# First mixer of a fused block: stick-breaking sums by a running total on VectorE, retention heads in pairs, gate products on one bank

## The reference, cut to what matters

```
# stick-breaking, 8 heads of 64, query blocks of 128
z = einsum('bthd,bshd->bhts', q, k) * scale
log_one_minus = where(s < t, log_sigmoid(-z), 0)
suffix = cumsum(log_one_minus, reverse=True) - log_one_minus
w = where(s < t, exp(log_sigmoid(z) + suffix), 0)
out = einsum('bhts,bshd->bthd', w, v)

# retention, 4 heads of 64 keys and 128 values
scores = einsum('bhnid,bhnjd->bhnij', rotary(q), rotary(k)) * decay
o = rms_norm(scores @ v + carried state) * silu(rg)
```

## Time and profile before

| | |
|---|---|
| Time, median of 3 runs | 2060.03 us (2060.03 to 2063.84) |
| Time of the profiled execution | 2062.9 us |
| Its span, first to last instruction | 2061.1 us |
| TensorE busy | 1815.9 us, 88% of the span |
| VectorE, ScalarE, GpSimd busy | 951.9, 740.2, 925.8 us |
| Share of the last-ended chain on TensorE | 71% |
| First mixer from the first `sz` to the last `sp` | about 99 to 330 us |

### The profile page before, as it was taken

The page is one execution under the profiler, slowest core; times in us unless marked ns, Lnnn a source line. Parts: engine busy times, 40 slices in busy tenths (PEclk is TensorE's granted clock), DMA queues, the critical chain, the costliest instruction groups (busy, mean ns, idle before and its releaser), DMA issues.

```text
span 2061.1 us, 20065 instructions
## 1 busy us (share of the span) xinstructions
PE 1815.9 (88%) x7492; PEld 1363.4 (66%) x7492; DVE 951.9 (46%) x1451; ACT 740.2 (36%) x1207; POOL 925.8 (45%) x1100
## 2 busy tenths in 40 slices
PE   5999889888878898878999999988777889999996
PEld 4776456666756576455788888755454568888885
DVE  1033333677562599754430323564755554123244
ACT  4253454445344422364332322342232342322232
POOL 3433113464753354113565656468222246565563
PEclk9999999998988899988999999998778899999998
DMA  4211102212111222012233323211000122333231
GB/s 167 92 62 52 41 21 73 70 62 72 50 33 34 69 80 74 21 31 72 73 95 99 102 93 102 82 62 51 11 11 21 31 64 90 103 92 102 93 94 70
DMA packets 39553, 139.90 MB, mean 68 GB/s; under 512 B 4512, under 2 KB 4640, under 8 KB 39328
## 3 DMA queue, kind: packets, MB, share of 16 engines
q1 hardware_dynamic: 39456, 138.61, 21.1%
HBM read 136.50 MB, written 2.10 MB: 67 GB/s over the span
## 4 chain that ended last, share of the span: by engine, by line
PE 71%; DVE 17%; ACT 7%; issue 2%; POOL 1%; DMA 0%; SPq 0%; DVEq 0%; ACTq 0%; POOLq 0%
PE ps L570 18%; PE ps L571 17%; PE ps L572 17%; DVE ps L1689 3%; PE ps L599 2%; PE ps L583 1%; PE ps L2101 1%; PE ps L585 1%; PE ps L584 1%; PE ps L818 1%; PE ps L820 1%; POOL wl L2586 1%; PE ps L2078 1%; ACT wh L624 1%; PE ps L811 1%
## 5 line engine op out<-in xcount | busy, mean ns | idle before, releaser
L2586 POOL TENSOR_TENSOR wl<-raw,wh 128x256 fp32r<-128x256 f32 x988 | 801.7, 843 | 998.7 <-ACT wh L624 990.8
L570 PE MATMUL ps<-hh,wh 128*128 128x512 f32 x1204 | 518.5, 431 | 70.2 <-DVE hl L687 45.8
L571 PE MATMUL ps<-hl,wh 128*128 128x512 f32 x1204 | 479.5, 398 | 0.0
L572 PE MATMUL ps<-hh,wl 128*128 128x512 f32 x1204 | 478.9, 398 | 0.0
L624 ACT ACTIVATE wh<-raw 128x1024 fp32r<-128x1024 f32 x247 | 261.1, 1058 | 554.8 <-PE ps L572 507.5
L570 PEld LDWEIGHTS ps<-hh,wh 128*128 128x128 f32 x1204 | 233.2, 194 | 149.1 <-DVE hl L687 51.8
L570 PE MATMUL ps<-mh,wh 128*128 128x512 f32 x632 | 267.6, 423 | 46.1 <-DVE ml L1324 6.5
L571 PEld LDWEIGHTS ps<-hl,wh 128*128 128x128 f32 x1204 | 232.7, 193 | 61.4 <-issue 17.7
L572 PEld LDWEIGHTS ps<-hh,wl 128*128 128x128 f32 x1204 | 232.1, 193 | 50.8
L571 PE MATMUL ps<-ml,wh 128*128 128x512 f32 x632 | 254.2, 402 | 0.0
L572 PE MATMUL ps<-mh,wl 128*128 128x512 f32 x632 | 253.9, 402 | 0.0
(11 more groups left out here) (464 smaller groups left out, 2297.2 us busy)
## 6 DMA issues: line engine op xcount, KB each, us to landing
raw<-in_w SPq DMA_DIRECT2D x247, 512.0 KB, 3.5
x<-in_x SPq DMA_DIRECT2D x8, 256.0 KB, 6.9
out<-x SPq DMA_DIRECT2D x8, 256.0 KB, 2.0
arena<-in_rope SPq DMA_DIRECT2D x3, 512.0 KB, 4.8
arena<-in_dec SPq DMA_DIRECT2D x1, 1024.0 KB, 11.6
mats<-in_mats SPq DMA_DIRECT2D x1, 576.0 KB, 7.8
arena<-in_lw SPq DMA_DIRECT2D x1, 512.0 KB, 3.8
arena<-in_levels SPq DMA_DIRECT2D x1, 448.0 KB, 4.5
```

Of the source, the lines that this page charges most:

```text
L570: e.matmul(ps[b][:], a, xh, start=first, stop=False)
L571: e.matmul(ps[b][:], a, xl, start=False, stop=False)
L572: e.matmul(ps[b][:], l, xh, start=False, stop=final).then_inc(pe.sem, pe.up(*step))
L2586: e.tensor_tensor(wl[:, n % NHL, cut(i, 2)], raw[:, n % NRAW, cut(i, 2)], wh[:, n % NHL, cut(i, 2)].bitcast(F32), SUB).then_inc(split.sem, ...
```

## The change

1. **Stick-breaking sums.** The -2^100 mask is added to z by VectorE, in the bank, before ScalarE reads it (step `sz`, two additions of 128 columns). Softplus moves into a step `sy` of its own and needs no mask. VectorE keeps the running sum of later key blocks (`later_at`: for n = 2 and 1 one addition and one copy for each lane, in step `ss`). TensorE then needs one `tri` matmul and, for n < 3, one `negones` matmul, and no mask matmul.
2. **Retention by pairs of heads.** `rz` issues both heads of a pair back to back, one on each half of the partitions, into banks 2 and 3; `rv` and `rn` issue both heads too, in banks 7 and 1.
3. **Gate products on one bank.** The `rg` groups all use bank 0, since bank 1 is now taken.
4. **Order.** The retention steps are laid by hand among the gate groups, each group's eviction stands before one more retention step, and the costs in `LONG` and the distances handed to `beside` are new.

```diff
-LONG = {"w": 0.69, "t": 2.8, "ra": 0.9, "rz": 0.6, "rv": 0.6, "rn2": 0.9}
+LONG = {"w": 0.69, "t": 2.8, "ra": 0.9, "rz": 0.5, "rv": 0.9, "rn2": 1.4}
...
-            stick += [[("sz", j, n)] + before, [("ss", j, n)]]
+            stick += [[("sz", j, n)] + before, [("sy", j, n)], [("ss", j, n)]]
...
-    return out + beside(others + part[:-10], stick, 5.4, 2.7) + before + part[-10:] + closing(4)
+    return out + beside(others + part[:-10], stick, 2.8, 2.6, 2.7) + before + part[-10:] + closing(4)
...
-    "even": {... "rg": (0, 1), ...},
+    "even": {... "rg": (0,), ...},
...
 # TensorE, step rz
-                    e.matmul(ps[b][:, 0:T - 128 * i], rqk[2 + j][r, cut(i)], rqk[j][r, 128 * i:T], start=True,
-                             stop=True).then_inc(pe.sem, pe.up(*step))
+                    for lane in range(2):
+                        r = slice(64 * lane, 64 * lane + 64)
+                        e.matmul(ps[2 + lane][:, 0:T - 128 * i], rqk[2 + j][r, cut(i)], rqk[j][r, 128 * i:T], start=True,
+                                 stop=True).then_inc(pe.sem, pe.up("rz", 2 * j + lane, i))
...
 # TensorE, step ss
-                        e.wait_ge(dve.sem, dve["masked", lane, j, n])
-                        e.matmul(z, M("tri"), sp[:, OFF[n]:OFF[n] + T - 128 * n], start=False, stop=False, skip_group_check=True)
-                        for n2 in range(n + 1, 4):
-                            e.matmul(z[:, 128 * (n2 - n):], M("negones"), sp[:, OFF[n2]:OFF[n2] + T - 128 * n2], start=False,
-                                     stop=False, skip_group_check=True)
-                        e.matmul(z[:, 0:128], R("ident"), R("sneg"), start=False, stop=True, skip_group_check=True).then_inc(
+                        e.wait_ge(dve.sem, dve["softplus", lane, j, n])
+                        m = e.matmul(z, M("tri"), softplus_at(lane, n), start=False, stop=(n == 3), skip_group_check=True)
+                        if n < 3:
+                            e.wait_ge(dve.sem, dve["later", lane, j, n] if n < 2 else dve["softplus", lane, j, 3])
+                            m = e.matmul(z[:, 128:], M("negones"), later_at(lane, n), start=False, stop=True,
+                                         skip_group_check=True)
...
 # VectorE
+                        z = ps[4 + lane][:, 0:128]
+                        e.tensor_tensor(z, z, M("sneg"), ADD).then_inc(dve.sem, dve.up("z_masked", lane, j, n))
...
-                        e.tensor_tensor(sp[:, 0:128], sp[:, 0:128], M("smask"), MUL).then_inc(
-                            dve.sem, dve.up("masked", lane, j, n))
+                            e.tensor_tensor(to[:, 128:], sp[:, 128:], later_at(lane, n), ADD).then_inc(
+                                dve.sem, dve.up("later_sum", lane, j, n - 1))
+                            e.tensor_copy(to[:, 0:128], sp[:, 0:128]).then_inc(dve.sem, dve.up("later", lane, j, n - 1))
...
 # ScalarE, step sz
-                        e.wait_ge(pe.sem, pe["z", lane, j, n])
+                        e.wait_ge(dve.sem, dve["z_masked", lane, j, n])
```

More of the change, by code:

```diff
@@ L737, in turned, with softplus_at, later_at @@
             return e_tmp[2 * (j % 2)], e_tmp[2 * (j % 2) + 1]
+        RVB = (7, 1)
+        def softplus_at(lane, n):
+            o = (768, 640, 128, 0)[n]
+            return spb[lane][:, o:o + T - 128 * n]
+        def later_at(lane, n):
+            o = (0, 384, 0)[n]
+            return spb[lane][:, o:o + T - 128 * (n + 1)]
         def scores(h, i):
@@ L780, in pe_even @@
                 elif kind == "rz":
-                    _, h, i = step
-                    b, j, r = 2 + i % 2, h // 2, slice(64 * (h % 2), 64 * (h % 2) + 64)
-                    claim(e, b)
+                    _, j, i = step
+                    claim(e, 2)
+                    claim(e, 3)
                     if i == 0:
                         e.wait_ge(dve.sem, dve["rotated", 2 + j])
-                    e.matmul(ps[b][:, 0:T - 128 * i], rqk[2 + j][r, cut(i)], rqk[j][r, 128 * i:T], start=True,
-                             stop=True).then_inc(pe.sem, pe.up(*step))
@@ L788, in pe_even @@
-                    busy[b] = (dve, ("rz", h, i))
-                elif kind == "rv":
[L790 to L796, removed]
-                elif kind == "rn2":
[L798 to L801, removed]
+                    for lane in range(2):
+                        r = slice(64 * lane, 64 * lane + 64)
+                        e.matmul(ps[2 + lane][:, 0:T - 128 * i], rqk[2 + j][r, cut(i)], rqk[j][r, 128 * i:T], start=True,
+                                 stop=True).then_inc(pe.sem, pe.up("rz", 2 * j + lane, i))
+                        busy[2 + lane] = (dve, ("rz", 2 * j + lane, i))
+                elif kind == "rv":
+                    _, j, i = step
+                    for lane in range(2):
+                        h, b = 2 * j + lane, RVB[lane]
+                        if i == 0:
+                            claim(e, b)
+                            e.wait_ge(act.sem, act["te", "rv", 3])
+                        e.wait_ge(dve.sem, dve["rz", h, i])
+                        e.matmul(ps[b][:, 128 * i:T], rv[:, i, cut(h)], scores(h, i)[:, 0:T - 128 * i], start=(i == 0),
+                                 stop=(i == 3)).then_inc(pe.sem, pe.up("rv", h, i))
+                elif kind == "rn2":
+                    for lane in range(2):
+                        h, b = 2 * step[1] + lane, RVB[lane]
+                        e.wait_ge(act.sem, act["rn_square", h])
+                        e.matmul(ps[b][:], M("ones"), scores(h, 1), start=True, stop=True).then_inc(pe.sem, pe.up("rn2", h))
+                        busy[b] = (act, ("rn_ln", h))
@@ L950, in act_even @@
                 elif kind == "rn1":
[L951 to L954, removed]
-                elif kind == "rn2":
[L956 to L961, removed]
+                    for lane in range(2):
+                        h, b = 2 * step[1] + lane, RVB[lane]
+                        e.wait_ge(pe.sem, pe["rv", h, 3])
+                        e.activation(oret[:, h, :], ps[b][:], ACT.Copy).then_inc(act.sem, act.up("rn_copy", h))
+                        e.activation(scores(h, 1), ps[b][:], ACT.Square).then_inc(act.sem, act.up("rn_square", h))
+                elif kind == "rn2":
+                    for lane in range(2):
+                        h, b = 2 * step[1] + lane, RVB[lane]
+                        e.wait_ge(pe.sem, pe["rn2", h])
+                        e.activation(scores(h, 0), ps[b][:], ACT.Ln, scale=1.0 / 128, bias=C(EPS)).then_inc(
+                            act.sem, act.up("rn_ln", h))
+                    for h in (2 * step[1], 2 * step[1] + 1):
+                        e.wait_ge(act.sem, act["rn_ln", h])
+                        e.activation(scores(h, 0), scores(h, 0), ACT.Exp, scale=-0.5).then_inc(act.sem, act.up("rn_exp", h))
                 elif kind == "ga":
```

76 lines of the change are left out of this document (48 added, 28 removed), and 2 rows, old and new, of the table BANKS.

## The result

| | median | runs | span of the profile |
|---|---|---|---|
| before, measured beside it | 2061.94 us | 2060.03 to 2068.16, 4 | 2061.1 us (the profile of the earlier trace rows) |
| changed kernel | 2041.46 us | 2040.97 to 2044.16, 4 | 2039.4 us |

The ratio is 0.9898, 95% interval 0.9882 to 0.9915: 21 us faster (17.5 to 24.3), where 13.3 were forecast. The median lies at the lower edge of the range, 2041; the ratio on the 2060.03 us that the forecast started from gives 2039.0, outside it. Between the profiles the gain is 21.7 us.

A forecast was written before the change was run, and what follows sets the result against it. TensorE, busy 211.4 of the first mixer's 231 us, was taken as the bound. Work of -16.1 us with changes in waits and clock summed to -13.3, so 2060.0 became 2046.7 us, range 2041 to 2054 (forecast's own 2043 to 2050).

The forecast's parts named there:

- (c): Value evictions: TensorE waits 3.9 us against 0.8 before, +3.1, and 2.3 more for a low clock behind them.
- (d): Retention norm sums: waits for squares 4.5 us instead of 6.8, decayed-score waits of 1.3 gone, -3.6; low clock stays.
- the tail: From the last gate product's eviction to the output projection: waits of 7.9 us against 5.8, +2.1.
- (a): Stick-breaking running sum: whole-sum and mask matmuls leave TensorE, 10.2 us less work, with 8 and 11.4 as ends.
- (b): Retention scores: two heads of a pair run at the same time on TensorE, 5.9 us less, at most 6.7.
- the bank: Output projection: TensorE's wait for an evicted bank, 1.6 us before, grows by the mask's 0.45.
- the blocked scores: One block of scores directly follows the sums that used its banks and waits for both exponentials, +0.7 us.
- the rotary waits: TensorE's waits for rotary inputs go, as these no longer queue on VectorE behind softplus, -2.4 us.
- evictions pace the pairs: Rival: retention pairs wait for VectorE's decay products to free their banks, 9.6 us, giving 2056.3; chance 0.09.
- no overlap: Rival: the two heads' retention scores run one after the other, 5.9 us not won, giving 2052.6; chance 0.06.
- the clock stays up: Rival: neither the 2.8 us eviction wait nor the 2.6 us squares wait lowers TensorE's clock, giving 2042.7; chance 0.16.
- the mask becomes the wait: Rival: VectorE reaches the mask 2 us late, so `ss` waits, 18 us in 16 blocks, giving 2064.7; chance 0.03.

The follow-up runs named there:

- evictions first: Changed kernel with the four value evictions placed ahead of a block of scores whose ScalarE passes stood before them; ratio to before 0.9882.
- squares first: Changed kernel with copies and squares of heads 0 and 1 ahead of a 512-column block of scores in ScalarE's queue; ratio to before 0.988.
- the run with the sum alone: Kernel before with only the new running sum and the mask on VectorE; order, banks and single heads stay; ratio to before 0.9955.
- the run with the pairs alone: Changed kernel with the old sums and mask products on TensorE; head pairs, one gate bank and new order stay; ratio to before 0.9957.
- the run on one half: Changed kernel with both score products of a retention pair reading the lower 64 partitions; ratio to before 0.9933.
- four such moves and two more banks: Changed kernel with value evictions and squares earlier, tail filled, one score block a value step later, four projection banks for two; 2028.79 us, ratio to before 0.9828.
- the first three moves alone: Changed kernel with value evictions earlier, squares earlier and the last wait before the output projection filled with other work; ratio to before 0.9839.

## Why the prediction was off

The direction, the bound and most of the waits were right. The size was 8.4 us short between the profiles (21.7 less 13.3) and about 7 by the medians. By its steps, as the difference to what was measured between the profiles:

1. **(c) and (d), the clock: 4.3 us, the step that failed.** I added 2.3 us for a new fall behind the evictions and kept the old one behind the squares, as prices tied to the length of a wait. The fall behind the evictions came (5.7 us of work at low clock, 2.9 lost), but the squares' fall did not, the stretch behind the first wait was half as long, and that behind the tail shorter: 2.0 us won instead of 2.3 lost. The second traces show that this sum is not a property of the kernel: 12.4 and 10.0 us for the changed one, 16.3 and 17.6 for the one before, with one stretch behind 0.78 us of wait. The 2.0 won are in part luck of the trace: evictions first and squares first, with the same work and fewer waits, spent 17.0 and 17.4 us at the low clock, no less than the kernel before. Work and waits alone make 19.0 + 1.6 = 20.6 us, and the ratios of the two measurements say 20 to 21; so on the mean of the runs, as far as this tells, the clock gave about nothing, and the step fails there by the 2.3 that it took away. The prediction had this as a rival worth 4 us at 0.16, and drew on the Trainium skill, which says that the number of matmuls run at the low clock differs from run to run (TensorE: Matmul & The Clock Gate; it stands under "What's actually happening", not in the section that the prediction names), but kept a fixed price as the likeliest. The traces agree with that page and not with the price.
2. **(a) and (b), the work: 2.9 us.** 10.2 was 10.8 in the run with the sum alone. 5.9 was 8.0 in the run with the pairs alone, more than its upper end of 6.7. The score products themselves fell from 11.2 to 5.7 us, by 5.5, near the forecast. What the prediction put at nothing is the rest of the queue: the weight steps, as many as before, took 144.1 us before and 141.9 with the pairs alone, and the value products 0.5 less. The new order breaks the weight steps up less often, into 47 runs instead of 56. In both traces the first matmul of such a run takes about 0.15 us longer than the 0.23 of one in the middle, and the last 0.05; nine runs fewer make about 1.8 of the 2.2 us. That is worked out from the rows; no run tried the order by itself.
3. **The waits: 2.1 us.** The tail (7.8 against 7.9), the bank (1.92 against 2.05), the blocked scores (0.78 against 0.7) and the rotary waits were right to 0.1. The evictions were forecast at 3.9 in two waits and cost 3.0: the second vanished, because the weight step in between ran at the low clock. In the second trace that step ran at full clock and the second wait came, 0.8, which makes 3.8, so this term was right and 0.9 of the miss belongs to the clock. In the first trace the step began at 204.94, the scores at 206.72, and the fourth eviction ended at 206.62:

```profile
204.20 2.42 ACT L990 ACTIVATE mh_scratch<-ps,small 128x512 f32<-128x512 f32 x4
```

```profile
204.94 0.80 PE L576 MATMUL ps<-hh,wh 128*128 128x512 f32 x1 [3.02 <-ACT mh_scratch L990]
...
206.72 2.08 PE L806 MATMUL ps<-arena 64*128 64x512 f32 x4
```

   The squares cost 3.3 instead of 4.5, 0.7 of it at the second pair, where I had too much in front.
4. **Outside the mixer** 0.7 us went the other way.

The rivals: *evictions pace the pairs* has no row (no wait of TensorE for L914, the decay product); *no overlap* falls with the run on one half; *the clock stays up* came true behind the squares and not behind the evictions; *the mask becomes the wait* falls, as the mask costs a third of a microsecond at waits that were there anyway. One slip in its numbers: eight weight steps of 0.69 are 5.5 us, not 6.4; no term of the sum uses it, and no wait for softplus came.

## What to carry to other kernels

Count a bound engine's waits from rows, for each of them came within 0.7 us of its forecast once the clock was the same. Count its work from start to start, and include what a new order does to the matmuls that stay: that was the 2 us left out here. Put the clock down as a spread and never as a fixed price per wait: between two traces of one kernel the loss to it differed by up to 1.2 us in the mixer and 5.2 in the rest. Take a second trace before explaining a few microseconds by the clock. Where a list of steps sets the order in all queues, an eviction placed behind another chain's passes is a wait that moving one line takes away: four such moves and two more banks won another 14 us on the changed kernel, the first three moves alone 12.

## What the runs showed of the hardware

VectorE's new operations between two places in SBUF take about one and a half to three and a half times as long when they begin while GpSimd is in an operation of its own; its operations on PSUM don't. In the changed kernel VectorE at two places, and GpSimd at the first (it has no row at the second):

```profile
117.88 0.75 DVE L965 COPY arena<-arena 128x128 f32<-128x128 f32 x1
118.55 0.83 DVE L963 TENSOR_TENSOR arena<-arena 128x128 f32<-128x128 f32 x1
...
213.26 0.22 DVE L965 COPY arena<-arena 128x128 f32<-128x128 f32 x1
213.39 0.28 DVE L963 TENSOR_TENSOR arena<-arena 128x128 f32<-128x128 f32 x1
```

```profile
117.07 2.90 POOL L2631 TENSOR_TENSOR wl<-raw,wh 128x256 fp32r<-128x256 f32 x4 [3.78 <-ACT wh L630]
```

A copy of 128 columns takes 0.22 us alone and 0.75 beside GpSimd, a sum 0.28 and up to 0.83. Of the 32 new sums and copies, 13 began inside a GpSimd operation and took 0.52 to 0.96 us, each ending 0.07 to 0.29 us after that operation did; the other 19 took 0.21 to 0.42. The mask addition on PSUM takes 0.50 for two of them at 112.56, while GpSimd is busy, as anywhere else. The Trainium skill says that VectorE and GpSimd share a port pair that one of them locks for a whole instruction (SBUF — State Buffer, "SBUF: two separate sides"); these rows agree. It cost nothing that shows here, as TensorE never waits for the running sum, and I had not weighed it.
